# A two-layer SSM and attention trunk: the adaLN product spread over the conv and feed-forward stages, norms summed block by block

## The reference

```python
c_act = silu(c)
ada = c_act @ w_ada[l] + b_ada[l]                 # 1024 x 6144 weights, one row of input
sh1, sc1, g1, sh2, sc2, g2 = split(ada, 6)
h = rms_norm(x, norm1_g[l]) * (1 + sc1) + sh1     # norm 1
z, xbc, dt_raw, q, k, v, gate_s, gate_a = split_cols(h @ w_in[l])
y_ssm = mamba2_branch(z, xbc, dt_raw, ...) @ w_ssm_out[l]   # causal conv of 4 taps + silu, then SSD by chunks
y_att = diff_attention_branch(q, k, v, ...) @ w_attn_out[l]
mixed = sigmoid(gate_s) * y_ssm + sigmoid(gate_a) * y_att
x = x + g1 * (mixed @ w_out[l])
h = rms_norm(x, norm2_g[l]) * (1 + sc2) + sh2     # norm 2
u = square(relu(h @ w_ff1[l]))
x = x + g2 * (u @ w_ff2[l])
```

## Time and profile before

| | us |
|---|---|
| median of 3 runs | 2994.64 (2994.18 to 3003.76) |
| the profiled execution | 3004.83, its span 3003.0 |
| TensorE busy | 2574.0, 86% |
| VectorE busy | 1322.4, 44% |
| GpSimd busy | 1086.1, 36% |
| ScalarE busy | 960.4, 32% |
| mean granted clock of TensorE | 0.914 of full speed |
| bytes moved | 251.56 MB, 84 GB/s |

### The profile page before, as it was taken

How to read it: one execution, slowest core, us unless ns; L and a number is a source line. 1 busy time by engine, 2 the same in 40 slices (tenths; PEclk the granted TensorE clock), 3 DMA queues, 4 the chain that set the end, 5 groups by cost and what they waited for, 6 DMA issues and landing times.

```text
span 3003.0 us, 36626 instructions
## 1 busy us (share of the span) xinstructions
PE 2574.0 (86%) x12200; PEld 2051.4 (68%) x12200; DVE 1322.4 (44%) x2019; ACT 960.4 (32%) x1532; POOL 1086.1 (36%) x825
## 2 busy tenths in 40 slices
PE   5798889788888697999977988988898877799997
PEld 2586667687666476888735866676776655688885
DVE  5654434332655326333366444433335552343333
ACT  1244332322544223222212443332334442232221
POOL 0244343334322144555402443433343222445552
PEclk9899989899989698999978999998999977899998
DMA  7421111122111121222273211011121111212221
GB/s 300 175 84 70 42 42 42 66 75 77 59 55 43 43 91 64 98 98 98 97 302 116 84 57 52 32 57 70 70 91 56 43 43 57 84 71 98 98 98 56
DMA packets 34516, 251.56 MB, mean 84 GB/s; under 512 B 3824, under 2 KB 4208, under 8 KB 4976
## 3 DMA queue, kind: packets, MB, share of 16 engines
q1 hardware_dynamic: 34416, 250.30, 22.8%
HBM read 244.00 MB, written 6.29 MB: 83 GB/s over the span
## 4 chain that ended last, share of the span: by engine, by line
issue 51%; POOL 23%; PE 11%; POOLq 9%; DVE 3%; DMA 2%; ACT 1%; DVEq 0%; PEld 0%; PEldq 0%; ACTq 0%; SPq 0%
POOL w_lo L1485 21%; POOLq L1487 7%; PE gemm L384 3%; PE gemm L385 2%; PE gemm L386 2%; PE aux L448 2%; DMA raw<-stream 2%; POOL y_tok L1526 1%; POOL smalls L1478 1%; DVE conv L1187 1%; POOL xdt L1517 1%; POOLq L1522 1%; PE aux L416 0%; POOLq L1518 0%; DVE pre L1090 0%
## 5 line engine op out<-in xcount | busy, mean ns | idle before, releaser
L1485 POOL TENSOR_TENSOR w_lo<-raw,w_hi 128x512 fp32r<-128x512 f32 x704 | 963.9, 1399 | 1590.0 <-ACT w_hi L732 1588.6
L384 PE MATMUL gemm<-h_hi,w_hi 128*128 128x512 f32 x1536 | 647.3, 421 | 37.9 <-POOLq L1487 10.1
L732 ACT ACTIVATE w_hi<-raw 128x2048 fp32r<-128x2048 f32 x176 | 336.6, 1914 | 939.9 <-PE gemm L386 849.3
L385 PE MATMUL gemm<-h_lo,w_hi 128*128 128x512 f32 x1536 | 614.1, 400 | 0.0
L386 PE MATMUL gemm<-h_hi,w_lo 128*128 128x512 f32 x1536 | 613.3, 399 | 0.0
L384 PEld LDWEIGHTS gemm<-h_hi,w_hi 128*128 128x128 f32 x1536 | 298.5, 194 | 135.5 <-issue 59.9
L384 PE MATMUL gemm<-op_hi,w_hi 128*128 128x512 f32 x896 | 362.4, 404 | 26.6 <-POOLq L1487 23.0
L385 PE MATMUL gemm<-op_lo,w_hi 128*128 128x512 f32 x896 | 359.5, 401 | 0.0
L386 PE MATMUL gemm<-op_hi,w_lo 128*128 128x512 f32 x896 | 358.3, 400 | 0.0
L385 PEld LDWEIGHTS gemm<-h_lo,w_hi 128*128 128x128 f32 x1536 | 298.8, 195 | 69.6 <-issue 12.0
L386 PEld LDWEIGHTS gemm<-h_hi,w_lo 128*128 128x128 f32 x1536 | 297.6, 194 | 65.4
(11 more groups left out here) (171 smaller groups left out, 2861.3 us busy)
## 6 DMA issues: line engine op xcount, KB each, us to landing
raw<-stream SPq DMA_DIRECT2D x200, 1024.0 KB, 4.8
ada_raw<-stream SPq DMA_DIRECT2D x24, 1024.0 KB, 7.2
xsave<-x SPq DMA_DIRECT2D x2, 2048.0 KB, 12.6
x<-xsave SPq DMA_DIRECT2D x2, 2048.0 KB, 7.8
x<-xT SPq DMA_DIRECT2D x1, 2048.0 KB, 7.7
out<-y_out SPq DMA_DIRECT2D x1, 2048.0 KB, 6.3
dtw_raw<-dtw SPq DMA_DIRECT2D x2, 512.0 KB, 8.0
rope_cos<-ropes SPq DMA_DIRECT2D x2, 256.0 KB, 2.7
```

The lines of the kernel that those rows point to most:

```text
L384: mm(o, w_hi[:, slot, k, cols], hi[:, k, :], start=k == 0, stop=False)
L385: mm(o, w_hi[:, slot, k, cols], lo[:, k, :], start=False, stop=False)
L732: A(w_hi[:, slot], raw[:, slot], ACT.Copy).then_inc(hi_ready, 1)
L1485: gp.tensor_tensor(w_lo[:, slot, ks], raw[:, slot, ks], w_hi[:, slot, ks].bitcast(F32), ALU.subtract)
```

## The change

- *Ahead of norm 1 of layer 0* only the 8 pieces of sh1 and sc1 are made, all by TensorE, with the weights as the stationary operand and c as one column (`ada_piece`, 16 products a piece). Each has its own buffer, so their loads go out at once, x, par and dtw after the first two. Squares of x are first on ScalarE.
- *12 pieces* (g1, sh2, sc2) go to VectorE in layer 0's conv stage, one after the silus of each unit (`early`), the sum over partitions on TensorE after the next unit (`ada_column`).
- *28 pieces* (g2 of layer 0 and all 24 of layer 1) go the same way into layer 0's feed-forward (`late`), one after each of its first 28 units.
- *SyncE* issues a unit's load and a piece's load by turns; a piece's load waits for VectorE's end (`ada_step`) of the piece two before.
- *Layer 1* starts without pieces; its squares are summed under the last ff2 units of layer 0, and the first conversion, w_lo, dtw and lambdas are taken ahead.
- *Norm sums, mixed, mix_hi and mix_lo* go block by block (semaphores xb, mixed). The output leaves in 8 issues of 256 KB. Units without a wait inside run column by column. The layer loop and the loops of bc, xs and feed-forward are written out on SyncE, TensorE and VectorE.

The core of the diff:

```diff
@@ sp_program
+            for n in range(N_FIRST):
+                piece(ada_pe[n], *FIRST[2 * n], pe_in[n])
+                piece(ada_first[n], *FIRST[2 * n + 1], first_in[n])
+                if n == 0:
+                    sp.dma_start(x[:], xT).then_inc(x_in, 16)
+                    load_par(0)
+                    load_dtw(0)
+            for l in range(DEPTH):
+                for n in range(U_GATE):
+                    unit(l, n)
...
+                    if l == 0:
+                        if n == 0:
+                            sp.wait_ge(ada_full, 1)
+                        elif n == 1:
+                            sp.wait_ge(aux_full[2], total_at(l, "start", "bank2", 0) + 1)
+                        else:
+                            sp.wait_ge(ada_step, step_at(n - 2))
+                        piece(ada_early[n % 2], *EARLY[n], early_in[n % 2])
...
+                for n in range(U_FF, UNITS):
+                    unit(l, n)
...
+                    if l == 0 and m < N_LATE:
+                        if m == 0:
+                            sp.wait_ge(S_["mixed"], total_at(l, "mix", "mixed", KB))
+                        if m >= 2:
+                            sp.wait_ge(ada_step, step_at(N_EARLY + m - 2))
+                        piece(ada_late[m % 2], *LATE[m], late_in[m % 2])
...
-            sp.dma_start(out, y_out[:]).then_inc(out_done, 16)
+            for k in range(KB):
+                sp.wait_ge(S_["pre"], DEPTH * TOTAL["pre"] + k + 1)
+                sp.dma_start(out[:, k], y_out[:, k]).then_inc(out_done, 16)
@@ pe_program
+            def ada_piece(where, bank, c):
+                for j in range(2):
+                    for k in range(KB):
+                        last = mm(bank[:, c + j:c + j + 1], where[:, k, j * P:(j + 1) * P], cact[:, k:k + 1],
+                                  start=k == 0, stop=k == KB - 1)
+            def ada_column(n, acc, bank, c):
+                pe.wait_ge(ada_step, step_at(n))
+                for j in range(2):
+                    last = mm(bank[:, c + j:c + j + 1], acc[:, n % 2, j * P:(j + 1) * P], ones[:, 0:1], start=True, stop=True)
+                last.then_inc(ada_out, 1)
...
                     for slot in range(2):
                         unit(l, i + U_BC // 2, slot, h_hi, h_lo)
+                        if i or slot:
+                            early(2 * i + slot - 1)
@@ dve_program
+            def ada_piece(n, where, landed, acc):
+                dve.wait_ge(*landed)
+                for k in range(KB):
+                    if k == 0:
+                        dve.wait_ge(ada_out, n - 1 + OUT_CREDIT)
+                        TS(acc[:, n % 2], where[:, 0], cact[:, 0:1], None, ALU.mult).then_inc(ada_step, 1)
+                    else:
+                        dve.wait_ge(ada_step, n * KB + k)
+                        STT(acc[:, n % 2], where[:, k], cact[:, k:k + 1], acc[:, n % 2], ALU.mult, ALU.add)\
+                            .then_inc(ada_step, 1)
...
                         if c % 2:
                             silu(step, c - 1, dst(c - 1))
                             silu(step, c, dst(c))
+                            early(2 * base + c // 2)
```

More of the change, by code:

```diff
@@ L296, in raw_at @@
         def raw_at(l, nh):
-            return (l * SLOT_LOADS + nh + 1) * 16
-        def sp_program(sp):
-            sp.dma_start(con[:], consts).then_inc(con_in, 16)
[L303 to L344, removed]
@@ L703, in mixed, with late @@
                     def mixed(k):
-                        if u == 0:
-                            pe.wait_ge(S_["mix_lo"], st("mix_lo") + 1)
-                    unit(l, U_WO // 2 + u // 2, u % 2, h_hi, h_lo, mixed)
-                norm(st)
-                with pe.Fori(0, 4) as i:
+                        pe.wait_ge(S_["mix_lo"], st("mix_lo") + 1)
+                    unit(l, U_WO // 2 + u // 2, u % 2, h_hi, h_lo, mixed if u == 0 else None)
+                norm_sum(st)
+                norm_spread(st)
+                def late(n):
+                    if n < 4:
+                        bank, c = ab[2], 2 * n
+                    else:
+                        bank, c = ab[3], 2 * LATE[n][1]
+                    ada_column(N_EARLY + n, late_acc, bank, c)
+                    if n == 3 or n == N_LATE - 1:
+                        pe.drain().then_inc(ada_full, 1)
+                for i in range(4):
                     sf = Step(l, "ff", i)
@@ L1064, in dve_program, with norm_add @@
             dve.drain().then_inc(ready, 1)
[L1066 to L1068 removed]
+            def norm_add(step, ks):
+                for k in ks:
                     dve.wait_ge(S_["sq"], step("sq") + 1)
@@ L1107, in dve_program, with dtw_low @@
                     .then_inc(S_["lam"], 1)
-                TS(cw[:], par[:, C_CW:C_CW + (CONV + 1) * CONV_BLOCKS], 0.5, None, ALU.mult)
-                TT(subg[:], par[:, C_SUB:C_SUB + 1], par[:, C_OML:C_OML + 1], ALU.mult)
+            def dtw_low(step):
+                dve.wait_ge(S_["dtw"], step.at("dtw", 0) + 1)
+                TT(dtw_lo[:], dtw_raw[:], dtw_hi[:].bitcast(F32), ALU.subtract).then_inc(S_["dtw"], 1)
+            for l in range(DEPTH):
+                st = Step(l, "start")
+                if l == 0:
+                    norm_add(st, range(KB))
+                    norm_mean(st)
+                    dtw_low(st)
+                    dve.wait_ge(par_in, 16)
+                    of_params(st)
+                    take_ada(1, l, ab[3], 0, 0, 2)
+                    scales(0)
+                else:
+                    norm_mean(st)
+                norm(st, lambda k: amul[:, k:k + 1], lambda k: ada_v[:, 0, k:k + 1])
                 dve.wait_ge(S_["lam"], st.at("lam", 1) + 1)
```

369 lines of the change are left out of this document (236 added, 133 removed).

## The result

The changed kernel takes 3097.85 us in the median of four runs (3081.68 to 3100.47), the kernel before 2994.85 beside it: slower, ratio 1.0326, 95% interval 1.0285 to 1.0366. The profiled execution took 3097.99, its span 3096.2.

What follows compares the result with a forecast made beforehand. TensorE, busy 86% of the span, was taken to bound the kernel, besides stretches at starts. Terms summed to +124.0 on the profiled 3004.83 us, 3128.8, less 10.2 for a median of 3118 us; range 3036 to 3160.

Steps and rivals of the forecast that it cites:

- rival of a fast start: Before layer 0's norm 1: TensorE's 256 one-column passes cost 0.111 us each, 27 us less, 3091 in all; chance 0.13.
- The loop through SyncE's queue: Layer 0's conv stage: raw loads queue behind piece loads awaiting VectorE; 21.95 us per unit, +109.2 us.
- One sign: Expected in the profile after: TensorE's share in layer 0's conv window near one half.
- Feed-forward: Layer 0's feed-forward with 28 pieces: same queue loop, 21.1 us per ff1 unit instead of 10.88, +152.7 us.
- Start of layer 0: Up to norm 1's first "pre": eight pieces by TensorE at the slow 0.216 us a pass, −22.4 us.
- the −49: Layer 0's start term if the 256 passes cost 0.111 us each, 28.4 us together, instead of the slow price.
- Norm 2, merging, end: Block-by-block sums and output: norm 2 −5.7 us per layer, merging −8.6 for both layers, end −9.0.
- the written-out loops: Layer, conv and feed-forward loops written out: more instruction fetching, taken at 0 us, bounds −3 and +15.
- layer 1's start: From layer 0's last update to layer 1's third unit: pieces gone, squares summed earlier, −86.5 us, nearly sure.
- The rival on the other side: Conv and feed-forward of layer 0: raw loads come in time, VectorE alone pays, −87 us, 2908; chance 0.07.

Runs made afterwards that it cites:

- ahead2: Changed kernel with SyncE issuing layer 0's conv and feed-forward unit loads two units earlier relative to the piece loads; 2891.55 us, ratio 0.9645.
- conv2: Changed kernel with unit loads two units earlier in layer 0's conv stage alone, feed-forward order kept; 3003.43 us in one run.
- ahead1: Changed kernel with unit loads one unit earlier relative to the piece loads; 2897.71 us in one run.
- before_layers: Kernel before with only the loop over the two layers written out on all five engines; 2976.53 us, ratio 0.9924.
- small: Changed kernel with each of the 40 spread pieces loading only its first block, 128 KB instead of 1 MB, VectorE's work kept; 3030.71 us in one run.

## Why the prediction was right

Forecast: 3118, slower by 4.1%. Measured: 3097.85, slower by 3.3%. By the number alone the rival of a fast start, 3091, is nearer; the first "pre" at 79.80 rules it out (its 28.4 us of passes would have put it near 54), and the loop is seen turn by turn.

- *The loop through SyncE's queue*: right, in place, in cause and nearly in length. Forecast 21.95 us a turn in the conv stage, measured 20.9. From the raw load's issue to its conversion 7.1 and 8.4 us went by turns, about the forecast's 7.7 (against the earlier trace rows's 4.8 for one); the stretch from conversion to silus was 8.97 (138.15 to 147.12), not the 9.85 read from the earlier trace rows. Over ten turns that makes 8.8 of the 11.9 us by which the term, 97.3 instead of 109.2, is smaller. ahead2, conv2 and ahead1 show that it is the queue, and that the lead of units counts as the prediction has it. One sign was wrong: TensorE is busy 70% of the conv window (179.04 of 255), not near one half, since its products are longer at the lower clock.
- *Feed-forward*: turns of 20.5, 20.4 and 21.8 (forecast 21.1), the rest of the first round 67.1 (66.7), the term +154.0 (+152.7).
- *Start of layer 0*: −23.9 (−22.4), at the price forecast, 0.214 us a pass against 0.216, and in the main for the reason forecast, the low clock. Here it did not fall during such passes, as it did in the earlier trace rows, but was low from the start: L458's run is at the 1.2 GHz level throughout, and the 1.00 printed there only says that there is no entry. At 1.00 a pass of this form takes 0.114, and the term would have been near the −49. The weights' rows don't matter to it: the passes of the earlier trace rows load one row of 128 columns, and took 0.111 at 1.00 as well. The rule of the Trainium skill ("TensorE: Matmul & The Clock Gate", Part 1: the gate goes by how busy TensorE has been) does not fit this run if busy is what the trace records: 52 us of 52, and still the lower level.
- *Norm 2, merging, end*: −5.8, −5.9, −9.8 (−5.7, −4.3, −9.0). The late one in norm 2 is GpSimd's w_lo, as forecast. The timeline of the kernel after, from the last update of x to "pre":

```profile
1184.57 0.75 DVE L1580 SCALAR_TENSOR_TENSOR x<-gemm,g1h,x 128x512 f32<-128x512 f32 x1 [4.44 <-PE gemm L441]
...
1187.91 4.92 POOL L1648 TENSOR_TENSOR w_lo<-raw,w_hi 128x512 fp32r<-128x512 f32 x4 [6.23 <-ACT w_hi L821]
...
1193.00 1.01 POOL L1641 TENSOR_TENSOR smalls<-smalls 128x4 f32<-128x4 f32 x1 [0.18 <-issue]
1194.06 2.07 PE L504 MATMUL aux<-con,smalls 128*128 128x128 f32 x8 [5.83 <-POOL smalls L1641]
1196.18 1.41 DVE L1229 SCALAR_TENSOR_TENSOR pre<-x,amul,aux 128x512 f32<-128x512 f32 x2 [7.74 <-PE aux L504]
```

  The sums over partitions are there at 1188.3, and GpSimd's rsqrt goes only when its w_lo ends: 11.6 us in all (12.3 forecast).
- *The step that was mis-sized*: the written-out loops, taken at 0 with bounds −3 and +15. The layer loop alone is worth 23 us (before_layers), outside my bounds and of the other sign than I feared: I looked for the price of fetching more instructions and had no row for what goes with a loop. It is in the attention stages (−5.8, −6.1, forecast 0, of which 2 each are run to run), in part of layer 1's start (−91.4 for −86.5) and in small change elsewhere. The 0.88 us of a conv turn is not the layer loop: before_layers still takes 9.83 from conversion to silus. It is on VectorE, whose conv loop the change wrote out as well. In the timeline of the kernel before the taps have gaps, six in 5.51 us (223.86 to 229.37), where the row at 140.76 above has six in 4.93 without one:

```profile
223.86 0.75 DVE L1187 SCALAR_TENSOR_TENSOR conv<-gemm,cw,conv 128x511 f32<-128x511 f32 x1 [4.60 <-ACT conv L791]
224.78 0.75 DVE L1187 SCALAR_TENSOR_TENSOR conv<-gemm,cw,conv 128x510 f32<-128x510 f32 x1 [0.18 <-issue]
```

  No run wrote that loop out alone, so this last step is likely and not shown. Together these make up most of the miss of 20 us between the medians; how much exactly stays open, since the stages vary by some us from run to run.
- *The rival on the other side*, a loop that doesn't bind, was 2908 in the forecast; ahead2 is that kernel, 2891.55; it has the written-out loops' gain, which the 2908 leaves out, and its feed-forward keeps 41, not 31.

## What to carry to other kernels

Before adding a load to a queue, write down what its wait depends on and which loads stand behind it; where the later load feeds the work that ends the wait, the two form a loop, and its length, not the sum of the added work, is the new time per step. One or two steps of lead in the order break the loop without added work, and counting turns tells how many are needed. For products of one column, count the columns of weights that each pass loads, and ask at which level of the clock they will run. A granted clock of 1.00 at the start of a program is to be checked against a product of known length before it is believed.

## What the runs showed of the hardware that I had not expected

- 256 one-column passes in a row, 55 us with TensorE recorded busy throughout, ran at the 1.2 GHz level; the 512-column products behind them reached the 2.4 GHz level (0.63 us each before 85.42 us, 0.39 after).
- A one-column pass in float32 follows the last after 0.114 us at granted clock 1.00 and 0.216 at 0.50, with 128x128 weights; with 1x128 weights 0.111 at 1.00. With 128x64 weights, at the lower level, it is 0.106 within one half and 0.082 to 0.088 in the mean.
- Writing the two layers out made the kernel before 0.8% faster, though its program grew; the instruction queue moved no more for it, 0.85 MB against 0.88; the kernel after, with more loops written out, moved 1.26. The page's row of before_layers:

```profile
q8 instruction: 52, 0.85, 0.1%
```

- A piece's seven steps take 3.61 us on VectorE beside an idle GpSimd and twice that beside w_lo. The timelines of VectorE and GpSimd in ahead2's feed-forward:

```profile
1194.97 7.33 DVE L1208 SCALAR_TENSOR_TENSOR late_acc<-ada_late,first,late_acc 128x256 f32<-128x256 f32 x7
...
1195.91 5.58 POOL L1655 TENSOR_TENSOR w_lo<-raw,w_hi 128x512 fp32r<-128x512 f32 x4 [6.38 <-ACT w_hi L828]
```

  w_lo is longer too, 5.58 for 5.03. Slack covered it here, and in a kernel with a full VectorE it would not.
- The ssd stage, the same code in all kernels, took 302 us (small, layer 1, granted clock 0.93) to 318 (the kernel after, layer 0, 0.89).
